# Four heads' attention probabilities turned in one group, and one weight unit's low part made by GpSimd, in a one-core hybrid block

## What is computed

```python
h = rmsnorm(x, norm1_w)
proj = einsum('bsd,dp->bsp', h, w_in)          # q, k, v | z, xbc, dt | mlstm q, k, v, o, i, f
y_att   = moba_attention(rmsnorm(q), rmsnorm(k), v)      # 8 heads of 64, one block of 256 keys: causal softmax
y_ssm   = mamba2_ssd(z, xbc, dt, ...)                    # width 1024, gated by silu(z), normed
y_mlstm = mlstm_chunkwise(...)                           # 4 heads of 128, gated by sigmoid(o)
x = x + concat(y_att, y_ssm, y_mlstm) @ w_out
x = x + (gelu(causal_conv(gate)) * val) @ w_down         # gate, val = rmsnorm(x) @ w_up
```

## Time and profile before

| | |
|---|---|
| runs | 405.85, 406.20, 406.28 us; median 406.2 |
| the profiled execution | 405.96 us, of which the span from first to last instruction is 403.8 |
| TensorE busy | 399.2 us, 99% of the span, granted clock 1.00 throughout |
| VectorE busy | 306.5 us, 76% |
| ScalarE busy | 258.5 us, 64% |
| GpSimd busy | 48.2 us, 12%, most of it before 77 us |
| DMA | 74.08 MB, mean 183 GB/s |

### The profile page before, as it was taken

The page is one execution under the profiler, slowest core; times in us unless marked ns, Lnnn a source line. Parts: engine busy times, 40 slices in busy tenths (PEclk is TensorE's granted clock), DMA queues, the critical chain, the costliest instruction groups (busy, mean ns, idle before and its releaser), DMA issues.

```text
span 403.8 us, 5997 instructions
## 1 busy us (share of the span) xinstructions
PE 399.2 (99%) x2247; PEld 344.5 (85%) x2247; DVE 306.5 (76%) x445; ACT 258.5 (64%) x359; POOL 48.2 (12%) x30
## 2 busy tenths in 40 slices
PE   8999999999999999999999999999999999999996
PEld 8998888888888888888888888888888888888885
DVE  3999887679585889979666678976777667776775
ACT  5979848785599866897536485556553565535540
POOL 3107964421011000000004000000000000000000
PEclk9999999999999999999999999999999999999999
DMA  8864763774554423246554355656535565355202
GB/s 295 314 264 153 261 265 123 297 226 152 212 189 134 181 104 117 99 173 238 186 182 154 111 203 209 208 209 208 183 136 207 201 208 208 127 210 187 100 0 104
DMA packets 12643, 74.08 MB, mean 183 GB/s; under 512 B 1336, under 2 KB 2768, under 8 KB 4432
## 3 DMA queue, kind: packets, MB, share of 16 engines
q1 hardware_dynamic: 12616, 73.81, 51.0%
q10 hardware_dynamic: 8, 0.00, 0.0%
HBM read 72.74 MB, written 1.07 MB: 183 GB/s over the span
## 4 chain that ended last, share of the span: by engine, by line
PE 98%; DMA 1%; DVE 1%; issue 0%; ACT 0%; DVEq 0%; ACTq 0%
PE pj L1544 27%; PE pj L1545 15%; PE pj L1503 8%; PE pj L1505 8%; PE pj L1504 8%; PE mx L1569 6%; PE mx L1504 6%; PE mx L1505 6%; PE mx L1503 6%; PE mx L1544 3%; PE mx L1566 2%; PE pj L1547 2%; PE mx L1545 1%; DMA x_pad<-in_x 1%; PE pj L1614 1%; PE pj L1620 0%
## 5 line engine op out<-in xcount | busy, mean ns | idle before, releaser
L1544 PE MATMUL pj<-hT,whi 128*128 128x512 f32 x468 | 163.5, 392 | 0.0
L923 DVE TENSOR_TENSOR wlo<-w_b,whi 128x2048 fp32r<-128x2048 f32 x55 | 125.9, 2290 | 47.7 <-ACT whi L456 47.7
L1545 PE MATMUL pj<-hT,wlo 128*128 128x256 f32 x496 | 139.1, 281 | 0.0
L456 ACT CAST whi<-w_b 128x2048 fp32r<-128x2048 f32 x63 | 120.3, 1909 | 26.9 <-PE pj L1505 21.3
L1544 PEld LDWEIGHTS pj<-hT,whi 128*128 128x128 f32 x468 | 87.6, 187 | 19.0
L1545 PEld LDWEIGHTS pj<-hT,wlo 128*128 128x128 f32 x496 | 93.6, 189 | 1.6 <-issue 0.5
L416 POOL TENSOR_TENSOR wlo<-w_b,whi 128x2048 fp32r<-128x2048 f32 x8 | 37.1, 4632 | 115.2 <-ACT whi L456 96.8
L839 ACT COPY st_b<-pj 128x512 f32<-128x512 f32 x22 | 12.9, 587 | 40.4 <-PE pj L1545 40.4
L1503 PE MATMUL pj<-whi,hT 128*128 128x512 f32 x96 | 38.1, 397 | 0.0
L1505 PE MATMUL pj<-whi,hT 128*128 128x512 f32 x96 | 37.4, 390 | 0.0
L1504 PE MATMUL pj<-wlo,hT 128*128 128x512 f32 x96 | 37.4, 390 | 0.0
(11 more groups left out here) (281 smaller groups left out, 593.0 us busy)
## 6 DMA issues: line engine op xcount, KB each, us to landing
w_b<-in_w_in SPq DMA_DIRECT2D x23, 1024.0 KB, 4.8
w_b<-in_w_up SPq DMA_DIRECT2D x22, 1024.0 KB, 4.7
w_b<-in_w_down SPq DMA_DIRECT2D x11, 1024.0 KB, 4.7
w_b<-in_w_out SPq DMA_DIRECT2D x8, 1024.0 KB, 4.8
seg_b<-ld_rows SPq DMA_DIRECT2D x4, 512.0 KB, 6.5
x_pad<-in_x SPq DMA_DIRECT2D x2, 512.0 KB, 3.7
w_b<-in_w0c SPq DMA_DIRECT2D x1, 512.0 KB, 6.5
Wm_b<-m_rows_d SPq DMA_DIRECT2D x1, 512.0 KB, 5.5
```

What stands on the lines that cost most here:

```text
L456: nc.scalar.copy(whi[:, slot, :], wraw[:, slot, :]).then_inc(s.hi_done, 1)
L923: nc.vector.tensor_tensor(wlo[:, slot, :], wraw[:, slot, :], whi[:, slot, :].bitcast(F32), ALU.subtract).then_inc(s.lo_done, 1)
L1544: ins = nc.tensor.matmul(ps, whi[:, slot, w], hT[:, k, :, :], start=k == 0, stop=False, skip_group_check=True)
L1545: ins = nc.tensor.matmul(ps[:, 0:T], wlo[:, slot, w], hT[:, k, 0, :], start=early, stop=k == KD - 1, skip_group_check=True)
```

## The change

It does four things.

1. `U_OUT` (unit 24) joins `POOL_UNITS`: its low part is made by GpSimd instead of VectorE.
2. TensorE turns heads 0 to 3 in one group behind unit 21, and makes the scores of heads 4 to 7 behind unit 22. Their waits follow: scores of heads 4 to 7 wait for the copies of the turned heads 0 to 3, whose banks they overwrite; the turning of heads 2 and 3 no longer waits for masks.
3. ScalarE copies all four turned heads ahead of the high part of unit 24, and takes the exponentials of heads 6 and 7 ahead of `att_hi` 0.
4. VectorE takes `m_gate` 1 ahead of its place at unit 24's low part, and the masks of heads 4 to 7 in a row after it.

```diff
-    POOL_UNITS = (5, 6, 7, 8, 9, 10, 12, U_FFN + 1)
+    POOL_UNITS = (5, 6, 7, 8, 9, 10, 12, U_OUT, U_FFN + 1)
@@ ScalarE @@
-            first_at(21, pT_copy, 0)
-            first_at(21, pT_copy, 1)
             at(21, z_low, 0)
             at(21, m_norm, 1)
             first_at(22, z_low, 1)
+            for h in range(4):
+                first_at(22, pT_copy, h)
             at(22, exp_table)
-            at(22, pT_copy, 2)
             at(22, z_low, 2)
-            at(22, pT_copy, 3)
             at(22, p_exp, 4)
             at(22, p_exp, 5)
+            at(23, p_exp, 6)
+            at(23, p_exp, 7)
             at(23, att_hi, 0)
             at(23, z_low, 3)
             at(23, att_hi, 1)
-            at(23, p_exp, 6)
-            at(23, p_exp, 7)
@@ VectorE @@
-            first_at(22, p_mask, 4)
-            first_at(22, p_mask, 5)
             first_at(22, z_sum, 1)
-            at(22, m_gate, 1)
+            first_at(22, m_gate, 1)
+            for h in range(4, AH):
+                at(22, p_mask, h)
             at(22, z_sum, 2)
-            at(22, p_mask, 6)
-            at(22, p_mask, 7)
             at(22, p_scale, 4)
             at(22, p_scale, 5)
@@ TensorE, s_out @@
-                elif h in (4, 5):
-                    pe.wait_ge(s.p_masked, h - 1)
-                elif h >= 6:
-                    pe.wait_ge(s.pT_copied, h - 5)
+                elif h >= 4:
+                    pe.wait_ge(s.pT_copied, min(h - 1, 4))
@@ TensorE, pT_out @@
-                elif h in (2, 3):
-                    pe.wait_ge(s.p_masked, h + 3)
@@ TensorE, table @@
             for h in range(4):
-                at(20 + h // 2 * 2, pT_out, h)
-                at(21, s_out, h + 4)
+                at(21, pT_out, h)
+                at(22, s_out, h + 4)
                 at(23, o_out, h)
                 at(24, pT_out, h + 4)
```

## The result

| | before | changed kernel |
|---|---|---|
| median of 6 runs each, same chip | 406.17 us (405.85 to 406.36) | 407.88 us (407.61 to 409.25) |
| ratio, 95% interval | | 1.0043 [1.0029, 1.0057] |
| the profiled execution, and its span | 405.96, 403.8 | 409.25, 407.3 |

The change costs 1.7 us: 0.43%, with the interval 0.29% to 0.57%, or 1.2 to 2.3 us.

The account below looks back on a forecast made before the run. TensorE, busy for 99% of the span, was taken to bound the kernel. Terms 0.0 + 0 + 1.5 + 0.3 = +1.8 us on the profiled 405.96 gave 407.8, or 408.0 for the median; range 406.0 to 408.4.

Parts of the forecast that it names:

- gain of one group of transposes: TensorE, two groups of six transposes made one of twelve: gain 0.00 us, bounds 0 and 0.1.
- TensorE waits ahead of the output matmuls: Last mask done at 167.0 while TensorE wants the output matmuls at 165.43: 1.5 us of waiting.
- and more at unit 24: ScalarE's exponential of head 7 precedes the copy of the first attention rows, which unit 24 awaits: another 0.3 us.
- The main step: Head 4's mask TENSOR_SCALAR on VectorE is held until GpSimd's low part ends at 162.9: +1.8 us, chance 0.60.
- Rival 1: At head 4's mask, the tiny TENSOR_SCALAR passes beside GpSimd: price 0, 406.2 us; chance 0.35 with rivals 3 and 4.
- Rival 2: TensorE's transpose groups cost more than their starts show: faster, 405.9 us at best; 0.05 including any unforeseen gain.
- Rival 3: Unit 22 waits for the sum of z: TensorE stands 0.2 us, 406.4; chance 0.35 with rivals 1 and 4.
- Rival 4: GpSimd's low part is held instead, ending some tenths after 162.9: 406.2 us; chance 0.35 with rivals 1 and 3.
- The argument from L959: A VectorE SBUF TENSOR_SCALAR, 408 ns against 684 for two tensors, uses both ways into SBUF, so the mask's waits for GpSimd.

Follow-up runs that it names:

- maxima in PSUM: The changed kernel with the masks' two row maxima written to spare PSUM columns, so the TENSOR_SCALAR reads PSUM; 406.20 us, ratio 0.9986.
- four pieces: The changed kernel with GpSimd's low part of unit 24 made in four subtractions of 512 columns; 405.89 us, ratio 0.9994.
- the run without the regrouping: The kernel before with only unit 24's low part given to GpSimd, the old order kept; 408.73 us, ratio 1.0046.
- the first experiment: The changed kernel, but VectorE makes unit 24's low part again, ahead of the four masks; 407.21 us, ratio 1.0015.
- mended version: The changed kernel with the mask's maxima in PSUM (406.20 us), or with GpSimd's low part of unit 24 in four subtractions (405.89 us).
- the run with GpSimd after the masks: The changed kernel with GpSimd's low part of unit 24 waiting until all eight heads are masked; 409.89 us, ratio 1.0094.
- the ten-forms kernel: A separate kernel computing nothing of the reference, run once: ten VectorE instruction forms, each alone and beside a GpSimd subtraction; no kernel time given.

## Why the prediction was right

It gave 408.0 us; the median is 407.88. Its steps, with the 0.18 us that this run was late from its start taken off every time of the trace:

| step | forecast | measured |
|---|---|---|
| gain of one group of transposes | 0.00 | 0.00 (maxima in PSUM, four pieces: added 0.00) |
| unit 22 starts | 152.4 | 152.30 |
| scores of heads 4 to 7 start | 158.1 | 158.05 |
| GpSimd's low part of unit 24 | 158.3 to 162.9 | 158.39 to 162.98 |
| first mask starts | 158.8 | 159.01 |
| TENSOR_SCALAR of head 4: due, ends | 160.0, 162.9 | 160.25, 163.01 |
| SyncE issues the load of unit 27 | 163 | 163.01 (163.19 in the trace), and nothing waits for it |
| last mask ends | 167.0 | 166.95 |
| TensorE waits ahead of the output matmuls | 1.5 | 1.66 |
| and more at unit 24 | 0.3 | 0.27, of which 0.03 is regained at once (0.04 with ScalarE's order of before, in the run without the regrouping) |
| sum | 1.8 | 1.90 in the trace; 1.7 [1.2, 2.3] by the medians |

**The main step held, and its rivals fell.** The stated range, 406.0 to 408.4, held both outcomes, so the time alone says little; the rows of the table do. Rival 1 (the tiny TENSOR_SCALAR passes) had a chance of 0.35 with 3 and 4 and is refuted by the 2.76 us; had it held, the kernel would have been as fast as before, which is what the runs with the maxima in PSUM and with four pieces give. One thing that spoke for it, that GpSimd runs long beside VectorE at 32 to 76 us without harm, was no evidence: in the trace of before, every VectorE instruction that starts beside those seven low parts reads PSUM. Rival 2, a gain by the groups, found none. Rival 3, a wait of unit 22 for the sum of z: the sum ends at 151.92 and the unit starts at 152.30. Rival 4, GpSimd held instead: GpSimd was first by 1.9 us and kept its 4.6.

**The argument from L959**, that 512 elements in 408 ns need both ways into SBUF, was an inference from one row. What it implied for two elements is now measured in four kernels, and the escape it suggested, a PSUM source, works (0.16 us). Why the engine behaves so no run here shows. The Trainium skill's rule in "SBUF — State Buffer", section "Who interferes with whom", was the stronger argument, and the traces agree with it in every form of it that was tried: the second to come is fully blocked (4.08 us for 0.16), and reductions and one-input instructions outside the two-port modes are not (the 42 reductions, the TENSOR_SCALAR from PSUM, the reciprocal). The Trainium skill asks in "VectorE: DVE Perf Modes", section "Mode 2×_2P", for an even outermost dimension, or an odd one equal in source and destination; 3 elements held (4.08 us) agree with that as 2 do.

**A small error that cost nothing.** The first mask came 0.2 us later than I had put it (I had allowed 0.7 from the first score matmul to the addition, and it took 0.96), and GpSimd 0.1 later. Since the end of the hold is set by GpSimd and not by when the instruction arrives, the 0.2 cost nothing.

**What the prediction did not see** is how densely such instructions lie. It treated the mask of head 4 as the place of the conflict, and called a start of GpSimd a matter of tenths. Moved 5 us forward or 6 us back, the same 4.6 us found another victim each time, at 2.16 and 2.68 us. It also took VectorE's 2.28 us to be worth nothing to TensorE; that is true against the kernel before, but with the masks in a row they are worth 0.91, as the first experiment shows.

Neither mended version is shown to beat the kernel before: 0.9986 [0.9971, 1.0001] and 0.9994 [0.9977, 1.0011]. From unit 23 on TensorE's starts are those of the kernel before, but for a constant 0.63 us in the first of them that arose in its first 15 us, so there is no gain to expect. Why medians and traces differ, by tenths here and by more than 1 us in the run with GpSimd after the masks, I leave open.

## What to carry to other kernels

Before work goes to an idle GpSimd, list what VectorE will issue during it, by form. Beside a GpSimd subtraction of two SBUF tensors, a float32 TENSOR_SCALAR or copy from SBUF to SBUF on two or more elements, and a product of two SBUF tensors, stopped until the end of GpSimd's current instruction, however small they were, while a PSUM source, a reduction or a reciprocal passed. Other forms were not tried. If one of them is on the way to the bounding engine, give it a PSUM source or cut GpSimd's instruction into pieces (four pieces of 1.3 us cost GpSimd 0.4 us more in all, and what is held then still hangs on the phase). And search a timeline for long instructions of small shape, by the maximum beside the median of a line, since a held instruction counts as busy.

## What the runs showed that I had not expected

- A TENSOR_SCALAR on one element per partition passes beside GpSimd (0.15 us), one on two or three takes 4.08. I had thought that an even count might decide.
- One pair of rows looks as if the exclusion works the other way round as well. In the last pair of the ten-forms kernel, VectorE's product of two SBUF tensors of 512 elements started at 70.61, before GpSimd's subtraction:

```profile
70.61 0.68 DVE L97 TENSOR_TENSOR s_out<-a,b 128x512 f32<-128x512 f32 x1
```

```profile
65.47 4.50 POOL L65 TENSOR_TENSOR g_out<-a,b 128x2048 f32<-128x2048 f32 x1 [1.28 <-DVE r_out L84]
70.77 4.87 POOL L65 TENSOR_TENSOR g_out<-a,b 128x2048 f32<-128x2048 f32 x1 [0.80 <-DVE r_out L84]
```

  VectorE kept its 0.68 us, and GpSimd took 4.87 where the ten before took 4.49 or 4.50. The lengthening, 0.37, is less than the 0.52 from GpSimd's start to VectorE's end; what GpSimd does in the rest the rows do not show, and the case occurred once.
- GpSimd gives way between two instructions that follow each other without a wait: with four pieces a waiting TENSOR_SCALAR got in at a seam. The pieces take 1.28 to 1.30 us for 512 columns, 2.37 and 2.40 for 1024 and 4.6 for 2048, so that a piece costs little more than its columns.
